# One hybrid decoder layer on eight cores: tiles 4 and 5 of x earlier for ScalarE, the last first-half products of four tiles alternated, and a reload of branch results ahead of a load of weights

## The reference

```python
h = rmsnorm(x, norm_pre[l])                       # (B, S, D)
proj = jnp.einsum('bsd,de->bse', h, w_in[l])      # (B, S, 7168)
xa, ga, u, vb, gb, q, gc = split_cols(proj, IN_SPLITS)
ya = pool_mixer(xa, pool_w[l], pool_scale[l]) * jax.nn.silu(ga)
yb = spatial_gating(u, vb, sgu_ln_g[l], sgu_ln_b[l], sgu_w[l], sgu_b[l]) * jax.nn.silu(gb)
yc = memory_cross_attention(q, k_m, v_m) * jax.nn.silu(gc)
y = jnp.concatenate([rmsnorm(ya, g_a), rmsnorm(yb, g_b), rmsnorm(yc, g_c)], axis=-1)
out = jnp.einsum('bse,ed->bsd', y, w_out[l])
x = x + rmsnorm(out, norm_post[l])
```

## Time and profile before

| | |
|---|---|
| median of 3 runs | 1259.5 us (1257.91 to 1259.72) |
| profiled execution | 1258.87 us |
| its span on the slowest core (core 3) | 1257.2 us |
| spans of the eight cores | 1251.3 to 1257.2 us |
| granted TensorE clock, mean by core | 0.995 to 0.997 |
| TensorE busy | 1220.3 us (97%), 6224 matmuls |
| VectorE, ScalarE, POOL busy | 39%, 38%, 17% |

### The profile page before, as it was taken

How to read it: one execution, slowest core, us unless ns; L and a number is a source line. 1 busy time by engine, 2 the same in 40 slices (tenths; PEclk the granted TensorE clock), 3 DMA queues, 4 the chain that set the end, 5 groups by cost and what they waited for, 6 DMA issues and landing times.

```text
span 1257.2 us, 17843 instructions; the slowest of 8 cores (1251.3 to 1257.2 us)
## 1 busy us (share of the span) xinstructions
PE 1220.3 (97%) x6224; PEld 582.0 (46%) x6224; DVE 488.0 (39%) x782; ACT 475.9 (38%) x892; POOL 216.0 (17%) x205
## 2 busy tenths in 40 slices
PE   6889999999999999999999999999989999999997
PEld 3345544444444455555554444444434444444443
DVE  4167624332232233444443233333222454343434
ACT  4377733422222232222225555555632232223222
POOL 1000001221211011111121111111222222222222
PEclk9999999999999999999999999999999999999999
DMA  9945322554234452645435541441975492533231
GB/s 210 245 152 173 69 81 68 105 90 83 50 67 81 83 93 45 107 88 91 97 63 98 86 82 34 81 88 34 178 212 138 129 307 75 178 133 118 93 109 68
DMA packets 50938, 137.83 MB, mean 110 GB/s; under 512 B 22785, under 2 KB 35201, under 8 KB 37137
## 3 DMA queue, kind: packets, MB, share of 16 engines
q0 software_dynamic: 7632, 50.86, 24.3%
q1 hardware_dynamic: 43218, 85.83, 21.3%
HBM read 153.39 MB, written 29.36 MB: 145 GB/s over the span
## 4 chain that ended last, share of the span: by engine, by line
PE 90%; DMA 3%; DVE 2%; ACT 2%; issue 1%; SPq 0%; DVEq 0%; POOLq 0%; POOL 0%; ACTq 0%
PE ps L279 89%; DMA mem_pages<-x 2%; DMA mem_pages<-y_scr 2%; PE ps L282 1%; ACT mem_pages L391 1%; DVE mem_pages L395 1%; DVE mem_pages L1155 0%; ACT mem_pages L1030 0%; SPq L291 0%; ACT L1030 0%; DVE stat L1025 0%; DVE mem_pages L1127 0%; DVE mem_pages L1035 0%; DVE mem_pages L545 0%; ACT stat L256 0%
## 5 line engine op out<-in xcount | busy, mean ns | idle before, releaser
L279 PE MATMUL ps<-mem_pages 128*128 128x512 bf16 (+2 forms) x5760 | 1195.7, 369 | 7.9 <-DMA mem_pages<-y_scr 4.0
L279 PEld LDWEIGHTS ps<-mem_pages 128*128 128x128 bf16 x5760 | 555.7, 98 | 630.5 <-issue 22.8
L713 POOL TENSOR_TENSOR mem_pages<-mem_pages 128x512 f32<-128x512 f32 x72 | 91.1, 1266 | 599.9 <-ACT mem_pages L706 597.3
L700 ACT ACTIVATE mem_pages<-mem_pages,small_c 128x512 bf16<-128x512 f32 x96 | 68.8, 716 | 275.4 <-DVE mem_pages L772 148.1
L1127 DVE SCALAR_TENSOR_TENSOR mem_pages<-ps,stat,mem_pages 128x512 f32<-128x512 f32 x128 | 96.0, 750 | 166.8 <-PE ps L279 144.4
L1135 POOL TENSOR_TENSOR mem_pages<-mem_pages 128x512 f32<-128x512 f32 x64 | 81.1, 1267 | 257.3 <-ACT jk L1132 257.3
L1132 ACT ACTIVATE jk<-mem_pages 128x512 bf16<-128x512 f32 x64 | 40.3, 629 | 224.0 <-DVE mem_pages L1127 224.0
L903 DVE TENSOR_TENSOR mem_pages<-mem_pages 128x526 f32<-128x526 f32 (+3 forms) x80 | 56.1, 701 | 100.8 <-ACT mem_pages L897 95.8
L762 DVE TENSOR_TENSOR mem_pages<-ps,mem_pages 128x512 f32<-128x512 f32 x32 | 22.1, 691 | 141.3 <-PE ps L279 141.3
L732 ACT ACTIVATE mem_pages<-ps 128x512 f32<-128x512 f32 x96 | 54.5, 590 | 22.8 <-PE ps L279 19.4
L748 DVE CAST mem_pages<-ps 128x512 bf16<-128x512 f32 (+1 forms) x24 | 14.4, 601 | 124.6 <-PE ps L279 121.4
(11 more groups left out here) (66 smaller groups left out, 422.9 us busy)
## 6 DMA issues: line engine op xcount, KB each, us to landing
mem_pages<-w_pages POOLq DMA_DIRECT2D x44, 1024.0 KB, 12.9
mem_pages<-x SPq DMA_DIRECT2D x32, 1024.0 KB, 7.8
out<-mem_pages SPq DMA_DIRECT2D x15, 1024.0 KB, 4.7
y_scr<-mem_pages SPq DMA_DIRECT2D x96, 128.0 KB, 1.9
mem_pages<-y_scr SPq DMA_DIRECT2D x12, 1024.0 KB, 14.6
mem_pages<-w_pages POOLq DMA_DIRECT2D x8, 512.0 KB, 19.7
mem_pages<-mem SPq DMA_DIRECT2D x2, 1024.0 KB, 6.2
mem_pages<-mem_norm SPq DMA_DIRECT2D x1, 1024.0 KB
```

What stands on the lines that cost most here:

```text
L279: return lambda e: e.matmul(out, lhsT=lhsT, rhs=rhs, start=start, stop=stop)
L700: P.op("act", lambda e: e.activation(out=yv, in_=tmp, func=AF.Copy, scale=gbr[:, c:c + 1]), reads=[tmp_b[i], gbr_b], writes=[ring_b[r]])
L713: P.op("pool", lambda e: e.tensor_tensor(out=accl_v if last else acc, in0=acc, in1=dst, op=ALU.add), reads=[dst_b, acc_b[tb]], writes=[acc ...
```

## The change

Three things are moved, and no instruction is added or taken away.

- At the beginning, the load of tile 4 of x waits for the first weight half to land (`("v", 0, 0)`, half 0) and no longer for the third (`("v", 0, 1)`, half 0). The load of tile 5 keeps its wait. In ScalarE's and VectorE's order `x_a(4)` stands ahead of the four first-half statistics `v_ln_half(tt, 0)`, and these come in two pairs, the second behind the copy of tile 4's first transposed half. `x_a(5)` stands ahead of all second-half statistics and no longer behind that of tile 1.
- The four groups of `v_mm(3, 1, ...)` are no longer in one row of two and a rest; they alternate with the last groups of tiles 0 to 2.
- In `out_q`, `y_load(0)` comes ahead of `wo_load(2)`, from block 12 on; `wo_load(2)` comes from block 13 on.

```diff
-    W2, W3, W4 = wbuf(("v", 0, 1)), wbuf(("v", 1, 0)), wbuf(("v", 1, 1))
+    W1, W4 = wbuf(("v", 0, 0)), wbuf(("v", 1, 1))
...
-    x_load(4, [W2[0].wtok])
+    x_load(4, [W1[0].wtok])
     x_load(5, [W4[0].wtok])
...
             v_mm(tt, 0, 1, part)
-            if part == 1:
-                v_ln_half(tt, 0)
     x_a(4)
+    for tt in range(2):
+        v_ln_half(tt, 0)
     drop(*VN, dyn=False)
...
     x_pe(4, (7, 7), (0,))
+    for tt in range(2, 4):
+        v_ln_half(tt, 0)
     v_mm(0, 1, 1, 0)
     v_mm(1, 1, 1, 0)
     x_pe(4, (7, 7), (1,))
+    x_a(5)
     v_mm(2, 1, 1, 0)
-    v_mm(3, 1, 0, 0)
-    v_mm(3, 1, 0, 1)
     for tt in range(3):
+        v_mm(3, 1, tt // 2, tt % 2)
         v_mm(tt, 1, 1, 1)
         v_ln_half(tt, 1)
         v_ln_end(tt)
-        if tt == 1:
-            x_a(5)
-    v_mm(3, 1, 1, 0)
     v_mm(3, 1, 1, 1)
     v_ln_half(3, 1)
     v_ln_end(3)
...
-    out_q = [(3, 0, lambda: wo_load(0)), (3, 0, lambda: wo_load(1)), (3, 0, lambda: wo_load(2)),
-             (3, 13, lambda: y_load(0)), (2, 0, gp_load)]
+    out_q = [(3, 0, lambda: wo_load(0)), (3, 0, lambda: wo_load(1)), (3, 12, lambda: y_load(0)),
+             (3, 13, lambda: wo_load(2)), (2, 0, gp_load)]
```

## The result

The changed kernel took **1266.53 us** (median of 4 runs, 1265.54 to 1267.11), the kernel before 1259.03 us on the same chip: a ratio of 1.006, 95% interval 1.0042 to 1.0077. It is slower by 7.5 us, where 1261.1 us was predicted, with 1264.0 as the upper end. The profiled execution took 1266.24 us. In the profiled execution of one later kernel, tail_gain_mid, four cores ran at a lower clock throughout, and only its cores 2 to 5 are read.

A forecast was written before the change was run, and what follows sets the result against it. TensorE, nine tenths of the chain, was taken as the bound, so only its idle or lower-clock time could be won. 1258.87 - 0.3 (beginning) + 2.5 (tail) = 1261.1 us, range 1253.2 to 1264.0.

The forecast's parts named there:

- Beginning, tile 4: Start of the kernel: tile 4 ready at 39.5 us, so TensorE's 4.49 us hole at 45.33 us goes.
- Beginning, what is late next: ScalarE waits for tile 5 until 56.8 us, statistics behind it; TensorE idles 9.9 us to 64.8, tile 6 at 78.0.
- The term of -0.3 us: Beginning's share of the sum: tile 6's transposes at 78.0 us against 78.30, 0.3 us won.
- Tail, the three waits for y_scr: Start of the output stage, from 909 us: TensorE's three waits for branch results, 4.0 us in all, go.
- Tail, who is late next: POOL's line 1135 waits for the gain (norm_post), and TensorE's line 722 waits for POOL, until 927.0 us.
- Tail, when the gain lands: Gain load issued at 906.84 us beside the weight load lands at 922.8 us, the middle of 920.0 and 925.6.
- both rows behind the ends: Trace rows bounding the gain: a 1 MB load behind stores took 13.2 us and landed 3.6 us after them, just after the weights.
- The lower end: Earliest gain landing in the tail: 906.84 + 13.2 = 920.0 us.
- The upper end: Latest gain landing in the tail, if it gets its way only when the weights are done: 922.0 + 3.6 = 925.6 us.
- The clock behind it: After 6.8 us idle ahead of line 722, TensorE runs at the lower clock: 1.7 us for eight matmuls.
- the second: Tail rival: gain held until the weights have landed, line 722 at 929.8 us, total 1263.9 us; chance 0.20.
- Rival 1: Tail: gain gets through between two weight pages, landed at 917.4 us, 4.6 us won there, total 1254.0 us; chance 0.25.

The follow-up runs named there:

- tail_gain_mid: Kernel before with y_load(0), wo_load(2), then the gain, held for the weights' first page, ahead of block 14's stores; last stores' page last among free pages: ratio 1.0029.
- front_x5_back: front_only with `x_a(5)` put back behind tile 1's second-half statistics; ratio 0.9973 to the kernel before.
- front_x5_load: front_only with the load of tile 5 waiting for the fifth weight half instead of the seventh; ratio 0.9957 to the kernel before.
- front_only: The changed kernel with `out_q` as before, so only the beginning is changed; ratio 1.0021 to the kernel before.
- tail_gain_pages: Kernel before with `out_q` ordered y_load(0), gain, wo_load(2), and the page of the last stores' source buffers last among the free pages; ratio 0.9950.
- tail_only: The kernel before with the changed kernel's new `out_q`, the beginning left as it was; ratio 1.0063 to the kernel before.

## Why the prediction was wrong, point by point

- **Beginning, tile 4:** right. `x_a(4)` at 35.2 us (34.2 to 35.4 over the cores, "near 34" predicted), and no hole at 45.3.
- **Beginning, what is late next:** right, and on core 3, whose rows it was made from, to 0.4 us: there `x_a(5)` came at 57.14 us (56.8 predicted), PE again at 65.16 (64.8), tile 6 at 78.03 (78.0). That the wait for tile 5 is the cause is shown by front_x5_back and front_x5_load. The term of -0.3 us was +0.2 in the mean of the cores, +1.2 from slowest core to slowest core, and up to +1.6 in front_only, so its range (-1.8 to +1.2) was a little short at the top. (The prediction's list of the holes leaves out a fourth, 2.37 us ahead of tile 5's transposes at 68.63 us; no term of the sum rests on it.)
- **Tail, the three waits for y_scr:** right, they are gone, and tail_gain_pages shows that they were worth 6.3 us.
- **Tail, who is late next:** right. POOL's line 1134 waits for norm_post, and line 721 for POOL.
- **Tail, when the gain lands: this step failed.** I took the middle of 920.0 and 925.6, "since both rows behind the ends are of this very pair of queues". It landed at 922.5 to 928.1 us by core, at 926.0 on core 3 and 928.1 on the slowest. The lower end was the worse one: its 13.2 us is of a load issued 9.5 us before the last page of its weights landed (882.1 + 23.3 against 895.9), while here 15.5 us of them were still to come (923.7 against 908.1). In that row the weights ended before the stores' turns did: by 903 us only 89 of their 256 packets had moved, and the rest needed no turns. Here all the 256 stood ahead of the gain while the weights ran. That count of turns is what the step lacked: it took the gain's landing from a row in which most of the stores' turns fell away with the end of the stream, and gave the stores no price of their own. The upper end had the right shape (last page, and some 4 us on), and was short for three small reasons on core 4: weights begun at 898.65 us and not 897.5, 25.0 us long and not 24.5, the gain 4.4 us behind them and not 3.6. That is 2.5 us, 925.6 + 2.5 = 928.1.
- **The clock behind it:** right in kind (0.50 behind the hole), and in size: 1.5 us of the difference between the spans lie behind line 721, and the ten matmuls' 4.42 us are 2.2 us more than ten at full clock, if no record of them is missing, against 1.7.
- **The choice of core:** all terms were made on core 3. On core 3 the span came out 5.2 us longer, or some 1264.1 us; core 4 was 2.2 us later still. Where a term differs by 5.6 us between cores, the slowest one has to be priced, not the one whose rows are at hand.
- **Rivals:** what happened is the second, at a chance of 0.20, and 2.6 us beyond its 1263.9 us. Its mechanism, as worded, isn't right: the weights as such don't hold the gain, since in tail_gain_mid a gain without stores ahead of it passed the last page. The turns of the two stores held it until then. Rival 1 was right that the queues take turns, and wrong that the turn comes between pages and that the stores ahead cost nothing.

## What to carry to other kernels

Before a load is moved beside another queue's stream, list everything that the second queue issues while the stream runs, and price it in packets and not in bytes, by the latest landing over all cores: here a store of 128 KB had as many packets as a load of 1 MB, and what stood behind two of them in their queue waited until the stream was over. Ask for what is wanted first ahead of the stream (here the gain, 6.3 us), and look at what the freed engine will then issue and whose pages it will want. Work that waits for a load should stand behind work that doesn't, unless its load comes early enough: with `x_a(5)` ahead of four statistics TensorE stood still for 10.2 to 11.3 us by core (front_only), behind them for 3.4 to 4.7 us at most (front_x5_back), and with the earlier load both places gave the same time within the intervals.

## What the runs showed of the hardware that I had not expected

- **Beside a weight load, the time to landing went by packets more than by bytes.** A tile of x of 1 MB took 11.6 and 12.5 us and 12.1 us in front_x5_load; a store of 128 KB took 11.3 and 11.8 us and 13.8 us in the changed kernel; the gain of 1 MB took 15.5 to 16.3 us in tail_gain_mid. The store and the gain are 128 packets each, and they took turns with the weights' packets one for one. With no weights under way such a store takes about 2 us (1.9 us at 895 us on core 4 of the changed kernel).
- **A second store behind the first costs its own turns as long as the stream runs.** On core 1 of tail_gain_pages the stores issued at 906.3 and 907.4 us landed at 919.6 and 927.2, with weights under way all the time. In the changed kernel they landed at 920.4 and 923.8, since the stream ended at 923.7.
- **The first packet came 3.8 to 4.8 us after the issue of the first store** over the cores of the changed kernel, and 0.8 us after it with no weights under way (core 4, 895.4 us). What it waits for wasn't tested.
- **In each pair of cores (0 and 1, 2 and 3, 4 and 5, 6 and 7) one got its gain clearly earlier:** in the changed kernel 923.9 and 926.7, 923.5 and 926.0, 922.5 and 928.1, 922.5 and 927.1 us; likewise in all four pairs of tail_only. It was always the one that had issued it earlier by its own clock, by 0.4 to 2.2 us, and it landed 1.8 to 5.9 us earlier. Its weights were done earlier too: in the changed kernel at 919.2 to 920.6 us on the four early cores and at 922.7 to 923.7 on the late ones. What the two share, and which of them is first, wasn't tested.
